# Value products of local and compressed keys on both column halves, their probabilities scaled by DVE

## The chip, the cores and the metric

The kernel runs on one core of one Trainium2 chip. The metric is the device time of one execution in microseconds. Before the change it is 1444.11 us, the median of three runs (1442.19 to 1448.04). Everything is float32.

## The reference

One step of a one-layer decoder for a prompt of 1024 tokens and a sample group of 8 times 4 tokens: an input projection, three kinds of heads side by side (forgetting attention or FoX, sparse attention, HGRN2), an output projection, a norm, and a mixture of experts. The change lies in the attention over the prompt. For each of 4 heads and each block of 128 queries the reference computes there:

```python
# forgetting attention: decay added to the scores, softmax, values
s = q @ k.T * scale + qc[:, None] - kc[None, :]      # causal
o_fox = softmax(s) @ v
# sparse attention: three branches with a gate each
o_c = masked_softmax(q @ kcmp.T * scale + bias) @ vcmp       # compressed keys, up to 63
o_s = masked_softmax(q @ ks.T * scale + bias) @ vs           # selected keys: here all blocks
o_w = masked_softmax(q @ kw.T * scale + bias) @ vw           # local keys: 640 columns at most
o_nsa = g_c * o_c + g_s * o_s + g_w * o_w
```

## The kernel before, in words

TensorE transposes, projects and multiplies; DVE adds biases and takes maxima; ScalarE takes exponentials and copies out of PSUM; GpSimd does some elementwise work and stores. The program of each engine is written out by hand, with semaphores between them.

The attention over the prompt is the stage "attn". It goes through a list of 64 pairs (`PAIRS`): for each head h (4) and each query block i (8), first the pair ("fox", "slc"), which has an even number d, then the pair ("win", "cmp"), which has an odd one. A pair goes through these steps:

1. `scores(d)` on TensorE (L853): products of queries and keys into the ring of four PSUM banks `vec`, at most 512 columns each.
2. `scores(d)` on DVE (L1795): bias added, row minimum taken, result into SBUF.
3. Exponentials on ScalarE (L1377), with their sums.
4. `normalise(d)` on DVE (L1805, L1807): sum times gate, reciprocal: two factors. The probabilities are multiplied by them, for even d by DVE (L1813), for odd d by GpSimd (L2204, which waits for the factors).
5. `transposes(d)` on TensorE (L865) into the three banks `turned`, in blocks of 128 keys.
6. Copies of the transposed probabilities to SBUF on ScalarE (L1370).
7. `values(d)` on TensorE: for even d FoX's products go to partitions 0 to 63 of the one bank `summed` (L877) and those of the selected keys to partitions 64 to 127 (L878), one after the other block by block. For odd d the blocks of local keys (L884, up to 5) and one of compressed keys (L886) are added to partitions 64 to 127 of the same bank.
8. After an odd d ScalarE copies the bank, both halves at once, into `QT` (L1357), and the bank is free.

The steps are staggered. TensorE issues in round d: scores(d), transposes(d-2), values(d-3). ScalarE issues in round d: for odd d-4 the copy out of `summed`, the copies of transposes(d-2), the exponentials of d. DVE issues scores(d), then normalise(d-1). In the round of block 4 of the first three heads TensorE (L841) and DVE (L1771) also make the next head's decay sums, from which GpSimd makes a tile with a mask (L2199) for the next head. The single bank `summed` holds the values of one query block: FoX's values of the next block wait until it has been emptied.

Below, "round E of i" is the even round of query block i, "round O of i" the odd one.

## Time and profile before

| | |
|---|---|
| median of 3 runs | 1444.11 us |
| the profiled execution's own time | 1449.1 us |
| its span, first to last instruction | 1447.0 us |
| TensorE busy in the span | 1304.1 us, 90% |
| the attention stage | about 626 to 891.4 us |
| TensorE, DVE, ScalarE, GpSimd busy in the stage | 240.5, 149.2, 150.8, 68.0 us |
| mean granted TensorE clock, span and stage | 0.94, 0.92 of full speed |

A matrix product of float32 shows as two records of TensorE, each with a weight load of its own. Records overlap at their ends, so the distance between starts says more of their price than their durations.

### The profile page before, as it was taken

To read this page: it belongs to the slowest core of one execution; us is meant where nothing else is said; L and a number is where in the kernel's file an instruction comes from. 1 tells how busy PE (TensorE), PEld (TensorE's weight loads), DVE (VectorE), ACT (ScalarE), POOL (GpSimd) and SP (SyncE) were. 2 spreads that over 40 slices of the span, in tenths; PEclk is the share of its full clock that TensorE was granted. 3 is DMA by queue.
4 is the path that set the end of the run, shared out by engine and by line. 5 is a ranking of instruction groups with operands and counts; after the bars stand their busy time and mean duration, and the time that the engine had idled before them with its cause. 6 is when DMAs were issued, how large, how long until landed. Compare 5 with 4: busy or idle time off the path is not lost.

```text
span 1447.0 us, 19519 instructions
## 1 busy us (share of the span) xinstructions
PE 1304.1 (90%) x6942; PEld 782.1 (54%) x6942; DVE 693.3 (48%) x1565; ACT 405.0 (28%) x858; POOL 237.3 (16%) x273
## 2 busy tenths in 40 slices
PE   3699999999999999878998999999937999999966
PEld 1468787777877555546666656544422333333322
DVE  5526574675744111256565553344762344433329
ACT  2232231422322010135655664222200111111016
POOL 0003021031211000212222222000001222211132
PEclk9799999999999999969999999999957999999988
DMA  9802020130201204306000002520057987595856
GB/s 305 247 26 59 17 73 1 31 59 17 72 2 46 95 9 79 99 12 167 25 21 5 1 1 84 161 80 30 29 199 248 316 287 258 177 319 158 291 177 225
DMA packets 123237, 163.18 MB, mean 113 GB/s; under 512 B 29763, under 2 KB 98547, under 8 KB 123160
## 3 DMA queue, kind: packets, MB, share of 16 engines
q1 hardware_dynamic: 108840, 112.75, 25.5%
q0 software_dynamic: 14320, 49.41, 9.8%
q8 instruction: 48, 0.79, 0.2%
q14 instruction: 29, 0.24, 0.1%
HBM read 225.01 MB, written 36.45 MB: 181 GB/s over the span
## 4 chain that ended last, share of the span: by engine, by line
PE 74%; DVE 16%; POOL 4%; DMA 2%; issue 2%; ACT 2%; SPq 0%; DVEq 0%; POOLq 0%; ACTq 0%
PE act L652 15%; PE vec L1159 11%; PE vec L919 9%; PE vec L681 7%; PE vec L702 4%; POOL arena L2204 3%; DVE arena L1795 3%; PE act L877 3%; PE vec L853 3%; PE act L865 3%; PE act L1172 2%; PE vec L1172 2%; PE vec L817 1%; DMA arena<-x_rows,arena 1%; PE vec L662 1%
## 5 line engine op out<-in xcount | busy, mean ns | idle before, releaser
L652 PE MATMUL act<-arena 128*128 128x352 f32 x768 | 239.1, 467 | 0.4 <-issue 0.4
L652 PEld LDWEIGHTS act<-arena 128*128 128x128 f32 x768 | 145.5, 193 | 77.0 <-issue 3.6
L1159 PE MATMUL vec<-arena 128*64 128x512 f32 x768 | 174.0, 605 | 2.6 <-issue 2.6
L1795 DVE CUSTOM_DVE_ANT_0 arena<-vec,arena 128x128 f32<-128x128 f32 (+9 forms) x200 | 86.8, 459 | 102.7 <-PE vec L853 92.8
L919 PE MATMUL vec<-arena 128*128 128x512 f32 (+1 forms) x288 | 127.8, 599 | 0.4 <-ACT arena L1357 0.4
L1159 PEld LDWEIGHTS vec<-arena 128*64 128x64 f32 x768 | 54.6, 138 | 105.2 <-issue 104.9
L681 PE MATMUL vec<-arena 128*128 128x512 f32 (+1 forms) x256 | 99.9, 546 | 0.0
L1370 ACT COPY arena<-act 128x512 f32<-128x512 f32 (+11 forms) x176 | 63.7, 431 | 105.1 <-PE act L865 105.1
L2204 POOL TENSOR_SCALAR arena<-arena 128x640 f32<-128x640 f32 (+4 forms) x64 | 59.2, 937 | 189.8 <-DVE arena L1807 189.8
L2089 DVE TENSOR_SCALAR arena<-arena 128x256 f32<-128x256 f32 x24 | 7.1, 296 | 172.4 <-ACT arena L1468 172.4
L853 PE MATMUL vec<-arena 64*128 64x512 f32 (+11 forms) x352 | 86.0, 486 | 3.2 <-DVE arena L1795 2.0
L919 PEld LDWEIGHTS vec<-arena 128*128 128x128 f32 (+1 forms) x288 | 51.4, 182 | 68.5 <-issue 66.9
L1377 ACT ACTIVATE arena<-arena 128x640 f32<-128x640 f32 (+15 forms) x128 | 81.5, 643 | 16.2 <-DVE arena L1795 16.1
L865 PE MATMUL act<-arena 128*128 128x128 f32 (+4 forms) x440 | 68.4, 294 | 19.3 <-POOL arena L2204 18.3
L681 PEld LDWEIGHTS vec<-arena 128*128 128x128 f32 x256 | 47.8, 190 | 44.9 <-issue 27.7
L865 PEld LDWEIGHTS act<-arena 128*128 128x128 f32 (+4 forms) x440 | 48.4, 145 | 41.7 <-POOL arena L2204 22.2
L1621 DVE COPY_PREDICATED arena<-arena,vec 128x512 f32<-128x512 int32 x64 | 44.5, 729 | 48.3 <-PE vec L702 46.5
L702 PEld LDWEIGHTS vec<-arena 128*128 128x128 f32 x512 | 61.9, 192 | 9.3 <-DVE arena L1604 3.2
L662 PE MATMUL vec<-arena 128*128 128x128 f32 (+1 forms) x576 | 65.3, 275 | 0.0
L662 PEld LDWEIGHTS vec<-arena 128*128 128x128 f32 (+1 forms) x576 | 64.5, 183 | 1.3
L702 PE MATMUL vec<-arena 128*128 128x128 f32 x512 | 62.7, 276 | 2.4 <-DVE arena L1604 2.4
L2227 POOL DMA_DIRECT2D y_rows<-arena x48 | 25.7, 539 | 229.1 <-DVE arena L2103 228.6
(379 smaller groups left out, 1902.3 us busy)
## 6 DMA issues: line engine op xcount, KB each, us to landing
arena<-in_exp_w SPq DMA_DIRECT2D x144, 1024.0 KB
y_rows<-arena POOLq DMA_DIRECT2D x48, 256.0 KB, 4.9
arena<-in_w_in SPq DMA_DIRECT2D x16, 512.0 KB, 7.1
arena<-in_x_prompt SPq DMA_DIRECT2D x8, 512.0 KB, 10.3
x_spill<-arena POOLq DMA_DIRECT2D x8, 512.0 KB, 6.0
arena<-x_spill SPq DMA_DIRECT2D x8, 512.0 KB, 5.5
arena<-in_cache_fox_kv SPq DMA_DIRECT2D x16, 256.0 KB, 3.5
x_rows<-arena POOLq DMA_DIRECT2D x8, 512.0 KB, 2.9
```

The source lines that it names most:

```text
L652: last = mm(bk[:, 0:n], W[k % 2][:, c, m * P:(m + 1) * P], xT[:, c, a:a + n], start=c == 0, stop=c == NC - 1)
L662: last = mm(bk[:r, o:o + P], xT[:, c, t * P:t * P + r], W[h % 2][:, c, 3 * P:4 * P], start=c == 0, stop=c == NC - 1)
L681: last = mm(bk[:r, 0:width], xT[:, c, t * P:t * P + r], w[:, c, 0:width], start=c == 0, stop=c == NC - 1)
L702: last = mm(bk[:, c * P:(c + 1) * P], a[:, ch], b[:, ch], start=True, stop=True)
L853: mm(bk[:, 0:n], QT[s, h, i * P:(i + 1) * P], k[:, first + a:first + a + n], start=True, stop=True).then_inc(*E.filled("vec"))
L865: last = e.transpose(bk[:n, c * P:(c + 1) * P], score_tiles(d)[j][:, (a + c) * P:(a + c) * P + n], ident)
L919: last = mm(bk[:r], src, Wo[:, c, half * 512:(half + 1) * 512], start=c == 0, stop=c == NC - 1)
L1159: last = mm(gu_bank[p][o], xgT[p][:, c, o], Wgu[:, slot, c, :], start=c == 0, stop=c == NC - 1)
L1370: e.copy(turned_tiles(d)[j][:w, a:a + k, :], bk[:w, 0:k * P].rearrange("p (c n) -> p c n", c=k)).then_inc(*E.drained("turned", ("pt", d, j)))
L1377: act(s, s, ACT.Exp, scale=-1.0, bias=sm_[:, least(i, kind, j):least(i, kind, j) + 1], accum_out=sm_[:, j:j + 1]).then_inc(*E.done(("exps" ...
L1795: ins = e.tensor_tensor_reduce(out=s[:, a + o:a + o + w], in0=bk[:, o:o + w], in1=bias, scale=1.0, scalar=prior, op0=ALU.add, op1=ALU.min, ...
L2204: e.tensor_scalar(s, s, small[:, d % 4, 2 + j:3 + j], None, ALU.mult).then_inc(*E.done(("probs", d)))
```

## The change

The value products of the local keys of an odd pair are parted. About half of them (`own`) stay on partitions 64 to 127 of columns 0 to 127; the rest and the product of the compressed keys go to partitions 0 to 63, columns 128 to 255, of the same bank, and the two kinds are issued in turns. ScalarE copies FoX's part into `QT` and the other half into a new SBUF tile on partitions 64 to 127, with two copies of 64 partitions. DVE then adds that tile to the bank's upper half into `QT` (`add_halves`), which empties the bank. DVE issues the addition at the start of each odd round, ahead of its scores. The scaling of the odd pairs' probabilities moves from GpSimd to the end of `normalise` on DVE.

```diff
--- before.py
+++ after.py
@@ -312,6 +312,7 @@
     PT = [z.take(1024, 8) for _ in range(2)]
     Sw = [[zc.take(640), zc.take(64)] for _ in range(2)]
     PTw = [zp.take(640, 5), zp.take(P, 1)]
+    other_half = zp.take(P)
     assert zc.at <= kept and zp.at <= shared
     assert z.at <= top, (z.at, top)
     attention_end = z.at
@@ -880,10 +881,16 @@
             else:
                 bk = E.banks["summed"][0]
                 first, L, nb = unit_keys("win", i)
-                for c in range(nb):
-                    mm(bk[64:128, 0:P], nkvg[:, first // P + c, 320:384], pt[0][:, c, :], start=False, stop=False)
                 n = unit_keys("cmp", i)[1]
-                mm(bk[64:128, 0:P], VC[:n], pt[1][:n, 0, :], start=False, stop=True).then_inc(*E.filled("summed", ("values", d)))
+                own = nb // 2 + nb % 2
+                upper = [(nkvg[:, first // P + c, 320:384], pt[0][:, c, :]) for c in range(own)]
+                lower = [(VC[:n], pt[1][:n, 0, :])] + [(nkvg[:, first // P + c, 320:384], pt[0][:, c, :]) for c in range(own, nb)]
+                for c in range(max(len(upper), len(lower))):
+                    if c < len(upper):
+                        last = mm(bk[64:128, 0:P], *upper[c], start=False, stop=c == len(upper) - 1)
+                    if c < len(lower):
+                        last = mm(bk[0:64, P:2 * P], *lower[c], start=c == 0, stop=c == len(lower) - 1)
+                last.then_inc(*E.filled("summed", ("values", d)))
 
         E.stage("attn")
         e.wait_ge(*E.at("KC ready"))
@@ -1354,7 +1361,8 @@
                 h, i, _ = PAIRS[d]
                 e.wait_ge(*E.full("summed"))
                 bk = E.job("summed")
-                e.copy(QT[:, h, i * P:(i + 1) * P], bk[:, 0:P]).then_inc(*E.drained("summed", "prompt attention done"))
+                e.copy(QT[0:64, h, i * P:(i + 1) * P], bk[0:64, 0:P]).then_inc(*E.done("fox outputs done"))
+                e.copy(other_half[64:128], bk[0:64, P:2 * P]).then_inc(*E.done(("other half", d)))
             d = it - 2
             if 0 <= d < n:
                 h, i, kinds = PAIRS[d]
@@ -1805,21 +1813,29 @@
             stt(sm_[:, 2:4], sm_[:, 0:2], TINY, skew(GI, 16 * i + 4 * h + 2 * (d % 2), [1, 2]), ALU.max, ALU.mult).then_inc(*E.done())
             e.wait_ge(*E.own())
             e.reciprocal(sm_[:, 2:4], sm_[:, 2:4]).then_inc(*E.done(("factors", d)))
-            if d % 2 == 0:
-                e.wait_ge(*E.own())
-                L = (i + 1) * P
-                for j in range(2):
-                    s = score_tiles(d)[j][:, 0:L]
-                    ts(s, s, sm_[:, 2 + j:3 + j], None, ALU.mult).then_inc(*E.done(("probs", d)))
+            e.wait_ge(*E.own())
+            for j, kind in enumerate(kinds):
+                s = score_tiles(d)[j][:, 0:unit_keys(kind, i)[1]]
+                ts(s, s, sm_[:, 2 + j:3 + j], None, ALU.mult).then_inc(*E.done(("probs", d)))
+
+        def add_halves(d):
+
+            h, i, _ = PAIRS[d]
+            e.wait_ge(*E.full("summed"))
+            bk = E.job("summed")
+            e.wait_ge(*E.at(("other half", d)))
+            tt(QT[64:128, h, i * P:(i + 1) * P], bk[64:128, 0:P], other_half[64:128], ALU.add).then_inc(*E.drained("summed", ("halves added", d), "prompt attention done"))
 
         n = len(PAIRS)
         decay_rows(0)
-        for it in range(n + 1):
+        for it in range(n + 4):
+            if it >= 4 and it % 2:
+                add_halves(it - 4)
             if it < n:
                 scores(it)
                 if it % 16 == 8 and it + 16 < n:
                     decay_rows(it // 16 + 1)
-            if it >= 1:
+            if 1 <= it <= n:
                 normalise(it - 1)
 
 
@@ -2197,11 +2213,6 @@
             if d % 16 == 9 and h + 1 < H:
                 e.wait_ge(*E.at(("cumf", h + 1)))
                 tt(foxdiag[(h + 1) % 2], cumf[(h + 1) % 2].rearrange("p (t k) -> p t k", t=8), C["diagmask"].unsqueeze(1).to_broadcast([P, 8, P]), ALU.add).then_inc(*E.done(("foxdiag", h + 1)))
-            if d % 2:
-                e.wait_ge(*E.at(("factors", d)))
-                for j, kind in enumerate(kinds):
-                    s = score_tiles(d)[j][:, 0:unit_keys(kind, i)[1]]
-                    e.tensor_scalar(s, s, small[:, d % 4, 2 + j:3 + j], None, ALU.mult).then_inc(*E.done(("probs", d)))
         E.stage("p5")
         e.wait_ge(*E.at("prompt attention done"))
         e.wait_ge(*E.at("kv_out"))
```

Two places in the order of the instructions. On TensorE, the end of round E and the start of round O of block 6 of head 2. Before: L853 are scores, L865 transposes, L884 and L886 the values of the local and compressed keys of block 4.

```order
L853 MATMUL vec<-arena 128x512 x2
L853 MATMUL vec<-arena 128x384 x2
L865 MATMUL act<-arena 128x128 x12
L884 MATMUL act<-arena 64x128 x5
L886 MATMUL act<-arena 64x128
```

Now, with L854, L866 for scores and transposes, L890 for the products on the upper half and L892 for those on the lower:

```order
L854 MATMUL vec<-arena 128x512 x2
L854 MATMUL vec<-arena 128x384 x2
L866 MATMUL act<-arena 128x128 x12
L890 MATMUL act<-arena 64x128
L892 MATMUL act<-arena 64x128
L890 MATMUL act<-arena 64x128
L892 MATMUL act<-arena 64x128
L890 MATMUL act<-arena 64x128
L892 MATMUL act<-arena 64x128
```

There are six products as before, now three for each half in turns.

On DVE at the same place, before: L1795 is scores(d) (its rows of 128x1 read out the row minimum), L1805 and L1807 make the factors, L1813 scales.

```order
L1795 ISA arena<-vec,arena 128x384
L1795 ISA arena 128x1
L1805 SCALAR_TENSOR_TENSOR arena<-arena 128x2
L1807 RECIPROCAL arena<-arena 128x2
L1795 ISA arena<-vec,arena 128x512
L1795 ISA arena 128x1
L1795 ISA arena<-vec,arena 128x55
```

Now, with L1803, L1813, L1815 and L1819 for the same four, and L1827 for the addition:

```order
L1803 ISA arena<-vec,arena 128x384
L1803 ISA arena 128x1
L1813 SCALAR_TENSOR_TENSOR arena<-arena 128x2
L1815 RECIPROCAL arena<-arena 128x2
L1819 TENSOR_SCALAR arena<-arena 128x640
L1819 TENSOR_SCALAR arena<-arena 128x47
L1827 TENSOR_TENSOR arena<-act,arena 64x128
L1803 ISA arena<-vec,arena 128x512
L1803 ISA arena 128x1
L1803 ISA arena<-vec,arena 128x55
```

Two scalings and the addition now stand in DVE's queue ahead of the scores of round O.

## Rows read from the trace of the kernel before

**Rows 1.** The page: span, then busy time, share and instructions of TensorE.

```profile
span 1447.0 us, 19519 instructions
...
PE 1304.1 (90%) x6942; PEld 782.1 (54%) x6942; DVE 693.3 (48%) x1565; ACT 405.0 (28%) x858; POOL 237.3 (16%) x273
```

**Rows 2.** Stretches: us, busy per engine, granted clock, DMA share, GB/s.

```profile
626.00:891.40 265.40, 240.45 (x1726) 165.88 (x1725) 149.24 (x623) 150.76 (x465) 68.03 (x69) 0.92 0.12 32
```

**Rows 3.** Waits of the stage: engine and line, releaser, us in total, times, longest.

```profile
DVE arena L1795 <- PE vec L853: 92.8, 61, 3.2
...
PE act L865 <- POOL arena L2204: 18.3, 24, 1.6
```

**Rows 4.** Timeline of TensorE: start, us, line, what.

```profile
769.41 0.92 PE L853 MATMUL vec<-arena 64*128 64x384 f32 x4
...
774.53 0.70 PE L853 MATMUL vec<-arena 64*128 64x512 f32 x2
...
803.82 1.78 PE L853 MATMUL vec<-arena 64*128 64x512 f32 x8
...
813.21 1.13 PE L853 MATMUL vec<-arena 64*128 64x512 f32 x4
...
816.95 1.32 PE L884 MATMUL act<-arena 128*64 128x128 f32 x10
...
818.55 1.57 PE L853 MATMUL vec<-arena 64*128 64x512 f32 x6
...
823.11 0.49 PE L853 MATMUL vec<-arena 64*128 64x128 f32 x4
```

**Rows 5.** Timeline of TensorE: three neighbouring value products, FoX and selected keys.

```profile
792.46 0.27 PE L877 MATMUL act<-arena 128*64 128x128 f32 x1
792.47 0.27 PE L878 MATMUL act<-arena 128*64 128x128 f32 x1
792.57 0.27 PE L877 MATMUL act<-arena 128*64 128x128 f32 x1
```

**Rows 6.** DVE's instructions of the stage by shape: busy us and mean ns.

```profile
L1813 DVE TENSOR_SCALAR arena<-arena 128x768 f32<-128x768 f32 x8 | 4.6, 619 | 0.1
L1813 DVE TENSOR_SCALAR arena<-arena 128x512 f32<-128x512 f32 x8 | 3.5, 485 | 0.1
...
L1813 DVE TENSOR_SCALAR arena<-arena 128x128 f32<-128x128 f32 x8 | 1.9, 286 | 0.1
```

**Rows 7.** GpSimd's instructions of the stage by shape.

```profile
L2204 POOL TENSOR_SCALAR arena<-arena 128x640 f32<-128x640 f32 x16 | 30.1, 1884 | 98.9 <-DVE arena L1807 98.9
...
L2204 POOL TENSOR_SCALAR arena<-arena 128x63 f32<-128x63 f32 x4 | 1.8, 460 | 0.0
```

**Rows 8.** By shape (DVE over the span): the nearest rows for a copy and an addition.

```profile
L1636 DVE SCALAR_TENSOR_TENSOR arena<-arena,vec 128x128 f32<-128x128 f32 x32 | 11.1, 348 | 11.3 <-PE vec L728 10.0
...
L1370 ACT COPY arena<-act 63x128 f32<-63x128 f32 x4 | 1.1, 267 | 0.0
```

**Rows 9.** Timeline of ScalarE: the copy out of the value bank, three times.

```profile
772.56 0.24 ACT L1357 COPY arena<-act 128x128 f32<-128x128 f32 x1
...
809.76 0.28 ACT L1357 COPY arena<-act 128x128 f32<-128x128 f32 x1
...
819.80 0.28 ACT L1357 COPY arena<-act 128x128 f32<-128x128 f32 x1
```

**Rows 10.** Timeline of DVE and GpSimd: two pairs of 640-column scalings.

```profile
791.36 2.76 DVE L1813 TENSOR_SCALAR arena<-arena 128x640 f32<-128x640 f32 x2
...
791.51 2.27 POOL L2199 TENSOR_TENSOR arena<-arena 128x1024 f32<-128x1024 f32 x1
...
853.76 1.02 DVE L1813 TENSOR_SCALAR arena<-arena 128x640 f32<-128x640 f32 x2
```

**Rows 11.** Stretches of 4 us around one fall of the clock.

```profile
776.00:780.00 4.00, 3.20 (x19) 1.87 (x17) 2.93 (x15) 2.44 (x8) 1.58 (x2) 0.99 0.00 0
780.00:784.00 4.00, 3.73 (x21) 2.19 (x20) 0.94 (x3) 1.63 (x6) 0.00 (x0) 0.59 0.00 0
```

## The prediction

> **What bounds the kernel now.** I read the page first. TensorE is busy for 1304.1 of 1447.0 us [rows 1], so a change pays where it takes work or waits off TensorE. Then I cut out the stage that is changed: in 265.4 us TensorE is busy 240.45, DVE 149.24, ScalarE 150.76 and GpSimd 68.03 us [rows 2]. TensorE is the bound there too, with 25 us in which it stands. The waits say for whom: 18.3 us in 24 waits of the transposes (L865) for GpSimd's scaling (L2204), 0.76 us each [rows 3]. In the same rows DVE waits 92.8 us for scores: it has spare time, and so has ScalarE [rows 2]. But both are links of a chain, so their durations count all the same. The last view is TensorE's timeline: it gives the length of a query block from round E to round E, 9.39 us for block 6 (803.82 to 813.21) and 9.90 for block 7 (813.21 to 823.11) [rows 4].
>
> **The value products.** With five blocks of local keys, L884 and L886 take TensorE from 816.95 to 818.55, 1.60 us for six products or twelve records [rows 4]. Where two column halves take turns, one record of each half starts every 0.11 us: L877 at 792.46 and again at 792.57, L878 at 792.47 [rows 5]. The new order is of that form. Six products make three turns of two records, 6 x 0.107 = 0.64 us. The product of the compressed keys uses fewer rows of the array than its neighbours. The twelve records at 0.107 would take 1.28 of the 1.60 us, and I give the other 0.32 to the two changes of form around it and keep it whole: 0.96 us. The gain is 0.64 us for a block, call it 0.62. Sixteen query blocks (i of 4 and more) have this form: 9.9 us. The smaller ones turn 5, 4, 3 and 2 products into 3, 2, 2 and 1 turns, some 0.4, 0.4, 0.2 and 0.2 us by the same working: 1.2 us a head, 4.8 in all. Together 14.7 us off TensorE. Bounds: 0 if the halves don't overlap, and 32 x 0.32 = 10 us more if the changes of form vanished too.
>
> The Trainium skill (TensorE: Matmul & The Clock Gate, Part 3) says that a weight load overlaps running products only where its row group differs. Here both halves use the same rows, so by that rule the turns would save nothing and the sum would lack its 14.7 us. The trace does not agree for this form: two loads and two products fit in 0.11 us.
>
> **The scaling.** GpSimd takes 1884 ns for 640 columns and 460 for 63, together 2.3 us [rows 7]. DVE takes 485 ns for 512 columns and 619 for 768 [rows 6]; for 640 I take the middle, 0.55 us, and for the compressed keys 0.24 (the 128-column row's 286 ns less some columns). The step on the chain shrinks from 2.3 to 0.8 us, 1.5 us less, and the wait is 0.76: it goes, 18.3 us. On DVE the 32 odd pairs cost 4 x (0.29 + 0.35 + 0.42 + 0.49 + 4 x 0.55 + 8 x 0.24) = 22.7 us, in an engine that idles 92.8 for scores. Its cover is thus there, except where something waits behind it in the queue, which comes next. So the most that the change can give is 14.7 + 18.3 = 33 us.
>
> **What is given back: the bank's way out.** The bank `summed` was emptied by one copy of ScalarE, which stands in its queue behind the exponentials of round E. Now two copies stand there and an addition on DVE. A copy with 63 partitions takes 267 ns [rows 8], so the two take 0.52 us. The addition (64x128, one operand in PSUM) isn't in the trace. It can't be less than nothing, since nothing leaves DVE for it, and the nearest row is an operation of two inputs, one in PSUM, on 128x128, 348 ns [rows 8]. I take 0.35 and 0.05 for the handover, as if half the partitions saved nothing. Then FoX's values of round O may begin, and behind them round E of the next block. That makes a loop: E starts, its scores, bias and exponentials pass, the copy begins, and E of the next block starts when copies, addition and values are through.
> - Block 7: the copy began at 819.80, 6.59 us after E [rows 4, 9]. Then 0.92 for copies and addition, 14 x 0.107 + 0.2 = 1.7 for FoX's values of block 6: 9.2 us, against 9.90 now and 9.90 - 0.62 - 0.76 = 8.5 if TensorE alone decided. Gain 0.7.
> - Block 6: 809.76 is 5.94 after E; + 0.92 + 1.5 = 8.35 against 9.39: gain 1.05.
> - Block 2: 772.56 is 3.15 after 769.41; + 0.92 + 0.6 = 4.7 against 5.12 (to 774.53): gain 0.4.
> - Blocks 0, 1, 3 and 5 I estimate from these: 1.1 for block 5, as in block 6; 1.0 for block 3, between its neighbours; 0.5 and 0.3 for blocks 0 and 1, which had no wait for GpSimd or next to none and in which only value products are saved.
>
> Without block 4 that is 5.05 us a head, 20.2 in all, where TensorE alone would allow 29 of the 33. DVE's own queue makes nearly the same loop (the scores of O now stand behind the addition, hence behind ScalarE's exponentials of E), so the two don't add.
>
> **Block 4.** In the first three heads GpSimd makes the next head's tile there (L2199). DVE's scalings of 640 columns began at 791.36, GpSimd's operation at 791.51 for 2.27 us, and the two scalings took 2.76 us; in the last head, without it, two took 1.02 [rows 10]. DVE stood still until GpSimd was through. Before, GpSimd's own scaling came first. Now its queue is empty, it starts as soon as the sums are there, and DVE's scaling of block 3's odd pair, 0.2 us later, waits for its end. The transposes of that pair come 0.5 us later than now instead of earlier, and the addition and the scores of O stand behind it. I take a loss of 0.5 us for each of three heads and a gain of 1.2 for the last: -0.3 in all.
>
> The Trainium skill (SBUF — State Buffer, Who interferes with whom) has the rule for it: a scaling on DVE in a two-port mode and a GpSimd operation lock each other out for a whole instruction. By that rule block 4 costs what I give it above, where an unhindered DVE would gain 1.2 us in each of three more heads, 5 us of the sum; rows 10 agree. The rule also says that an operation with at most one SBUF input is free of it, so the addition would not wait; no row here shows that.
>
> **The sum.** 20.2 - 0.3 - 0.6 (at the end of the stage the output projection waits for the second copy and the addition) = 19.3, say 19. What follows the stage starts from it and shifts whole. The profiled execution took 1449.1 us: 1430.1. The median of the runs was 5.0 us lower: 1425.
>
> **Rivals.**
> - *TensorE decides everywhere.* If the copies and the addition hide, 33 us come: 1411. For it: ScalarE and DVE are busy little more than half of the stage. Against: the loop's lengths above.
> - *The new loop is longer than I have it.* The exponentials of E start later because DVE is late from the round before; 0.4 us more in each of 32 blocks takes 13 us: gain 6, 1438. For it: DVE gets 22.7 us of scaling and 32 x 0.35 = 11 us of additions.
> - *The halves do not overlap*, since the compressed keys' product uses other rows. 18.3 us of waits go, less what the loop takes, and 8 us are left: 1436. Against: rows 5.
> - *Slower: the clock.* The granted clock was 0.59 from 780 to 784, after 3.20 us of 4 busy from 776 to 780 [rows 11], which is the lower level (1.2 GHz) for most of 4 us and costs 1.7 us of work at full speed. The packed products leave TensorE with fewer of them and more of it as transposes. Were there one more in each of 28 blocks, 48 us would be lost against 33 won: 1459. It decides from 11 more on. Against: the long gaps in front of it go.
>
> **How the numbers follow.** Forecast 0.60, TensorE alone 0.10, longer loop 0.13, no overlap 0.11, clock 0.06. A measurement here tells some 0.5% (7.2 us, so 1436.9) from no change. Faster: 0.60 + 0.10 + a third of the longer loop's 0.13 + half of the 0.11 = 0.80. Slower: 0.06. The rest, 0.14, is the same. The range reaches from TensorE alone (1411) to the longer loop (1438): 1412 to 1438, with the clock's case and the ends of the others outside.
>
> **What would show it.** In the profile after: no scaling on GpSimd in the stage and no wait of the transposes for it; the records of the two halves starting in couples 0.11 us apart; DVE busy 178 us there or a little less; a wait of FoX's values or of DVE's addition for ScalarE's copies; block 6 at 8.3 us; a long scaling on DVE beside GpSimd's tile in three heads; a stage of some 246 us instead of 265. I am wrong if the records of the halves start one by one, if the stage keeps its length, or if the mean clock in it falls under 0.90.

## The result

| | before | after |
|---|---|---|
| median, us | 1443.69 (4 runs, 1442.19 to 1448.04) | 1430.45 (4 runs, 1422.10 to 1431.61) |
| ratio, 95% interval | | 0.9891 (0.9848 to 0.9934) |
| profiled execution, us | 1449.1 | 1430.46 |

The changed kernel is faster by 1.1%. Timed again beside the last experiments, on one chip with them, the ratio was 0.9897 (0.9880 to 0.9914). The forecast was 1425 us, in a range of 1412 to 1438. The range held the time, and the ratio stands for 16 us where 19 were forecast.

The page of the kernel after: span and TensorE's line, as [rows 1] of before.

```profile
span 1428.5 us, 19615 instructions
...
PE 1289.3 (90%) x6942; PEld 765.9 (54%) x6942; DVE 721.5 (51%) x1661; ACT 414.8 (29%) x890; POOL 177.7 (12%) x209
```

The span is 18.5 us shorter. The stage now goes from 626 to 873 us (TensorE's first product of the output projection starts at 872.96, before at 891.37). This row of the stretches answers to [rows 2]: length, busy time of TensorE, weight loads, DVE, ScalarE and GpSimd, granted clock, DMA share, GB/s.

```profile
626.00:873.00 247.00, 226.75 (x1724) 150.65 (x1722) 176.95 (x717) 160.79 (x497) 8.04 (x5) 0.95 0.13 34
```

18.4 of the 18.5 us are in this stage. DVE is busy 177 us where 178 were forecast. The clock is 0.95 where it was 0.92. Next the waits of the same stretch, as [rows 3]: total us, times, longest.

```profile
PEld act L866 <- DVE arena L1819: 23.3, 25, 2.0
DVE arena L1827 <- ACT arena L1365: 22.4, 15, 4.0
...
DVE arena L1803 <- PE vec L854: 13.7, 16, 2.5
...
PE act L866 <- DVE arena L1819: 9.9, 8, 1.8
```

GpSimd's scaling is gone from the list; one wait of DVE for GpSimd, 2.1 us, is there before and after. DVE waits 13.7 us for scores instead of 92.8, and has a new wait: 22.4 us of its addition for ScalarE's second copy. TensorE's transposes wait 9.9 us, for DVE, where they waited 18.3 for GpSimd. Their weight loads (PEld) are idle as long as before, 23.3 against 22.2 us, yet only 8 of these 25 times do the products stand too (24 of 24 before). Of the 9.9 us, 5.5 lie in block 4 of the first three heads and 2.8 in block 0 of the last three.

The length of a block is the distance between the scores of two even rounds. These rows are TensorE's timeline of head 2 (the heads count from 0), as [rows 4]: the even rounds of blocks 6 and 7, the first of FoX's value products in block 7, then the even round of the next head's block 0 and its transposes.

```profile
789.77 1.78 PE L854 MATMUL vec<-arena 64*128 64x512 f32 x8
...
798.28 1.99 PE L854 MATMUL vec<-arena 64*128 64x512 f32 x8
...
805.95 0.29 PE L878 MATMUL act<-arena 128*64 128x128 f32 x1 [0.25 <-DVE arena L1827]
...
807.64 0.49 PE L854 MATMUL vec<-arena 64*128 64x128 f32 x4
809.00 1.20 PE L866 MATMUL act<-arena 128*128 128x128 f32 x9 [0.86 <-DVE arena L1819]
```

Block 6 takes 8.51 us (789.77 to 798.28), forecast 8.35; block 7 takes 9.36, forecast 9.2. In block 7 the value products stand 0.25 us for the addition; in block 6 TensorE stands for nothing. And in the last row TensorE stands 0.86 us for the scaling of block 7, which no rival of mine had in this place. The way out of the bank in the same blocks, first ScalarE's copies (as [rows 9]), then DVE's additions with what they waited for:

```profile
795.72 0.26 ACT L1364 COPY arena<-act 64x128 f32<-64x128 f32 x1
796.00 0.26 ACT L1365 COPY arena<-act 64x128 f32<-64x128 f32 x1
...
804.87 0.26 ACT L1364 COPY arena<-act 64x128 f32<-64x128 f32 x1
805.15 0.26 ACT L1365 COPY arena<-act 64x128 f32<-64x128 f32 x1
```

```profile
796.36 0.29 DVE L1827 TENSOR_TENSOR arena<-act,arena 64x128 f32<-64x128 f32 x1 [1.16 <-ACT arena L1365]
...
805.51 0.29 DVE L1827 TENSOR_TENSOR arena<-act,arena 64x128 f32<-64x128 f32 x1 [1.53 <-PE act L866]
```

The copies begin 5.95 and 6.59 us after the even round, as before (5.94 and 6.59). The addition ends 6.88 us after the round in block 6, forecast 5.94 + 0.92 = 6.86. In block 7 it ends at 805.80 and the first value product starts at 805.95: this second handover of 0.15 us has no term in the forecast, and it is nearly all that the two blocks are longer than forecast (0.16). The engine named last in such a row is not always the one that released: at 805.51 it is the copy that ended at 805.41.

The value products of five blocks of local keys and the compressed ones, in the last block of the last head:

```profile
866.25 0.43 PE L890 MATMUL act<-arena 128*64 128x128 f32 x2
866.61 0.43 PE L892 MATMUL act<-arena 55*64 55x128 f32 x2
866.97 0.32 PE L890 MATMUL act<-arena 128*64 128x128 f32 x1
866.97 0.32 PE L892 MATMUL act<-arena 128*64 128x128 f32 x1
867.13 0.27 PE L890 MATMUL act<-arena 128*64 128x128 f32 x1
...
867.56 0.33 PE L866 MATMUL act<-arena 128*128 128x128 f32 x1
```

The first couple does not overlap: two records of L890, then from 0.36 us later two of L892 with 55 rows, again 0.36 us, and only then couples, 0.16 and then 0.11 us apart, as [rows 5]. Six products take 1.31 us (866.25 to 867.56), before 1.60, forecast 0.96 to 0.98.

DVE's new operations (shape, count, busy us and mean ns, as [rows 6, 8]) and one of three meetings with GpSimd, as [rows 10]:

```profile
L1819 DVE TENSOR_SCALAR arena<-arena 128x640 f32<-128x640 f32 x24 | 12.9, 553 | 0.7
...
L1819 DVE TENSOR_SCALAR arena<-arena 128x512 f32<-128x512 f32 x12 | 10.2, 880 | 0.3
...
L1827 DVE TENSOR_TENSOR arena<-act,arena 64x128 f32<-64x128 f32 x32 | 9.5, 296 | 38.0 <-ACT arena L1365 22.4 <-PE act L866 11.2 <-PE vec L854 4.3
```

```profile
716.77 2.21 DVE L1819 TENSOR_SCALAR arena<-arena 128x512 f32<-128x512 f32 x2
...
716.55 2.00 POOL L2215 TENSOR_TENSOR arena<-arena 128x1024 f32<-128x1024 f32 x1 [60.45 <-DVE arena L1813]
```

640 columns take 553 ns (forecast 0.55), the addition 296 (taken as 350), but two scalings that should take 0.64 us take 2.21 beside GpSimd's tile, until it ends.

**All blocks.** I took the block lengths of every head from TensorE's scores, as above. Where the clock doesn't fall inside them they repeat to 0.02 us from head to head, with two exceptions after: block 0 takes 8.02 in head 1 and 7.85 in the next two, block 5 7.95 in head 1 and 8.04 in the last. In this table are those undisturbed lengths of heads 1 to 3 in us; block 4 is that of the last head, which has no tile and no sums. A star marks a length with a stretch at the lower clock in it, for want of another.

| kernel | 0 | 1 | 2 | 3 | 4, last head | 5 | 6 | 7 | 4, other heads |
|---|---|---|---|---|---|---|---|---|---|
| before | 7.21 | 4.10 | 5.12 | 6.27 | 8.41* | 8.88 | 9.39 | 9.90 | 11.83* and more |
| after | 7.85 | 4.05 | 4.91 | 5.71 | 6.89 | 8.0 | 8.51 | 9.37 | 11.13 |
| scaling by DVE alone | 7.22 | 4.10 | 4.32 | 5.40 | 6.69 | 8.03 | 8.79 | 9.33 | 11.12 |
| value part alone | 7.31 | 4.04 | 5.13 | 6.27 | 8.46* | none | 9.39 | 9.90 | 10.89 |
| after, addition behind the scores | 7.06 | 4.53 | 4.94 | 6.33 | 7.51 | 8.74 | 9.31 | 9.87 | 12.96* |
| after, early copies | 7.05 | 3.89 | 4.37 | 5.54 | 6.62 | 7.96 | 8.50 | 9.04 | 12.30* and more |
| after, late tile | 7.85 | 4.03 | 4.91 | 5.72 | 6.89 | 7.95 | 8.51 | 9.37 | 9.55 |
| scaling by DVE, late tile | 7.22 | 4.10 | 4.32 | 5.40 | 6.69 | 8.03 | 8.79 | 9.33 | 9.55 |
| after, all three edits | 7.03 | 3.73 | 4.37 | 5.20 | 6.47 | 7.60 | 8.35 | 8.89 | 9.55 |

From before to after, blocks 0 to 3 and 5 to 7 gain 2.5 us a head, 10 us in four. Three things correct this.

- Block 4: the 8.41 us of the last head before have 1.5 us at the lower clock in them. Less half of that they are 7.66, an estimate, and the gain is 0.8. In the other heads the same working gives 10.8 to 10.9 before against 11.13 after, a loss of some 0.3 in each of three.
- The stage's end: from the last even round on it takes 19.36 us where it took 18.03. It loses 1.3 us where block 7's gain of 0.5 stands in the 10. The transposes of the last odd pair wait 1.28 us for DVE's scaling there.
- The first two blocks of head 0 run at the lower clock and gain 0.4 together where the table has a loss of 0.6.

That leaves some 9 of the 18.4 us. The rest is the clock, told below.

### The profile page after: what moved, and what is told of

Read it like the earlier page. It is cut to its first block, busy times and chain, and to the rows that moved or that the text cites. A ratio compares the mean times of both kernels' runs of the same rounds, so it can differ in the third digit from the quotient of the medians.

```text
span 1428.5 us, 19615 instructions
## 1 busy us (share of the span) xinstructions
PE 1289.3 (90%) x6942; PEld 765.9 (54%) x6942; DVE 721.5 (51%) x1661; ACT 414.8 (29%) x890; POOL 177.7 (12%) x209
## 4 chain that ended last, share of the span: by engine, by line
PE 77%; DVE 14%; DMA 3%; ACT 3%; issue 2%; POOL 0%; SPq 0%; DVEq 0%; POOLq 0%; ACTq 0%
PE act L653 15%; PE vec L1166 11%; PE vec L926 9%; PE vec L682 7%; PE vec L854 5%; PE vec L703 4%; PE act L866 4%; PE act L878 2%; PE act L1179 2%; PE vec L1179 2%; DMA arena<-x_rows,arena 2%; PE vec L818 1%; PE act L890 1%; PE vec L663 1%; PE act L1146 1%
## 5 line engine op out<-in xcount | busy, mean ns | idle before, releaser
L1803 DVE CUSTOM_DVE_ANT_0 arena<-vec,arena 128x128 f32<-128x128 f32 (+9 forms) x200 | 86.8, 459 | 25.3 <-PE vec L854 13.7
L854 PE MATMUL vec<-arena 64*128 64x512 f32 (+11 forms) x352 | 84.2, 477 | 2.3 <-DVE arena L1803 1.8
L866 PE MATMUL act<-arena 128*128 128x128 f32 (+4 forms) x440 | 66.3, 288 | 10.9 <-DVE arena L1819 9.9
L866 PEld LDWEIGHTS act<-arena 128*128 128x128 f32 (+4 forms) x440 | 47.2, 142 | 31.9 <-DVE arena L1819 23.3
L854 PEld LDWEIGHTS vec<-arena 64*128 64x128 f32 x352 | 42.5, 197 | 33.4 <-issue 18.3
L1476 ACT ACTIVATE arena<-vec 128x256 f32<-128x256 f32 x24 | 9.3, 386 | 165.9 <-PE vec L1166 165.9
## 6 DMA issues: line engine op xcount, KB each, us to landing
arena<-in_x_prompt SPq DMA_DIRECT2D x8, 512.0 KB, 10.2
```

The lines of the kernel that those rows point to most:

```text
L854: mm(bk[:, 0:n], QT[s, h, i * P:(i + 1) * P], k[:, first + a:first + a + n], start=True, stop=True).then_inc(*E.filled("vec"))
L866: last = e.transpose(bk[:n, c * P:(c + 1) * P], score_tiles(d)[j][:, (a + c) * P:(a + c) * P + n], ident)
L1803: ins = e.tensor_tensor_reduce(out=s[:, a + o:a + o + w], in0=bk[:, o:o + w], in1=bias, scale=1.0, scalar=prior, op0=ALU.add, op1=ALU.min, ...
```

## The experiments

The theories: A, the one on record, that the wait for GpSimd is won and the longer way out of the value bank limits the gain; B, that the packed value products bring it; C, that a large part is the clock. The code below is shortened; what each line does stands in the text around it.

### Each part alone

The first kernel has DVE's scaling only (GpSimd's goes, as in the change; the line that scales stays as it was):

```diff
-            if d % 2 == 0:
-                e.wait_ge(*E.own())
-                L = (i + 1) * P
-                for j in range(2):
-                    s = score_tiles(d)[j][:, 0:L]
+            e.wait_ge(*E.own())
+            for j, kind in enumerate(kinds):
+                s = score_tiles(d)[j][:, 0:unit_keys(kind, i)[1]]
```

> The kernel before with one part of the change: DVE scales the probabilities of the odd pairs; value products, the single copy and GpSimd's empty queue otherwise as before. Theory A (the forecast's: the wait for GpSimd is what the change takes away): the 18.3 us of waits go, block 6 takes 8.9 us instead of 9.39, block 7 9.4 instead of 9.90, time 1430 to 1434. Rival B (the packed value products bring most): 1440 or more. Rival C (most of the gain is the clock, which falls less often when the waits are gone): 1430 too, but blocks without a fall gain under 0.4 us each and the stage shows 3 falls or fewer instead of 7.

It took 1421.51 us, ratio 0.9871 (0.9847 to 0.9895). TensorE's even rounds of blocks 5, 6 and 7 in the last head:

```profile
829.21 1.56 PE L853 MATMUL vec<-arena 64*128 64x512 f32 x8
...
837.24 1.78 PE L853 MATMUL vec<-arena 64*128 64x512 f32 x8
...
846.03 1.99 PE L853 MATMUL vec<-arena 64*128 64x512 f32 x8
```

Block 5 lasts 8.03 us, block 6 8.79 and block 7 9.33 (in the table), the last two 0.1 less than theory A has them. The time is 9 us lower than I expected of A. Some 4 us of that lie ahead of the stage, where the kernels are the same: in this trace its first product starts at 622.2 us, in that of the changed kernel at 626.4. A stage read from a trace is thus a better measure than the time when kernels of different series are compared, and it says more here: 264.7 us before, 246.5 with the whole change, 241.8 with the scaling alone. Of rival C's two conditions one holds and one does not: the stage has a single fall of the clock (counted as told below), but undisturbed blocks 2, 3, 5, 6 and 7 gain 0.6 to 0.9 us each too. Both theories hold a part.

The second kernel has the rest: value products on both halves, two copies, the addition, and GpSimd's scaling.

```diff
+            if d % 2:
+                e.wait_ge(*E.at(("factors", d)))
+                for j, kind in enumerate(kinds):
+                    s = score_tiles(d)[j][:, 0:unit_keys(kind, i)[1]]
+                    e.tensor_scalar(s, s, small[:, d % 4, 2 + j:3 + j], None, ALU.mult).then_inc(*E.done(("probs", d)))
```

> The other part alone: value products on both halves with two copies and DVE's addition, the odd pairs still scaled by GpSimd. Theory A: TensorE comes earlier to transposes that wait for GpSimd anyway, so the waits grow by what the products save and the longer way out of the bank costs a little: 1440 to 1448. Rival B (products bring most): 1434 or less. Rival C (clock): falls as often as before, 7 in the stage, and 1440 to 1446.

1444.55 us, ratio 1.0011 (0.9991 to 1.0030): nothing, as A said, and B falls. C's numbers hold nearly as well as A's (8 falls of the clock where 7 were named). Its transposes still wait for GpSimd (from 640 to 830 us):

```profile
PE act L866 <- POOL arena L2222: 15.1, 17, 1.6
```

So all the gain is in the scaling, and the value part on top of it takes some back. The two ratios with and without it (0.9891 and 0.9871) don't tell this apart, the block lengths do: in the table 1.2 us a head between those rows and 0.2 more in the last head's block 4, 5 us in all (blocks 0, 2 and 3 pay 1.5, block 6 wins 0.28 back). The stages of the two traces differ by 4.8 us. With a later edit in both kernels (the late tile, below) the ratios tell it too: 0.9842 (0.9816 to 0.9868) against 0.9774 (0.9755 to 0.9793).

### The product with fewer rows

```diff
-                lower = [(VC[:n], pt[1][:n, 0, :])] + [(nkvg[...], pt[0][:, c, :]) for c in range(own, nb)]
+                lower = [(nkvg[...], pt[0][:, c, :]) for c in range(own, nb)] + [(VC[:n], pt[1][:n, 0, :])]
```

> The changed kernel with the product of the compressed keys last among those on the lower half instead of first. In the changed kernel this product and its neighbour on the upper half run one after the other. If its odd number of rows costs a change of form on either side, putting it last takes one of them away: L890 and L892 together take 1.1 us for a block instead of 1.3. Theory A (the way out of the bank sets the length of a block): the time doesn't move beyond 1 us, blocks 6 and 7 stay at 8.5 and 9.4. Rival (TensorE's own work sets it): 0.2 us in each of 28 blocks, 5 us.

1423.85 us, ratio 0.9883 (0.9856 to 0.9910), not told apart from the changed kernel's by these intervals. Six products now take 1.16 us (853.01 to 854.17 in its trace) against 1.31, and blocks 6 and 7 stay at 8.50 and 9.36: less work of TensorE does not shorten them. It does shorten blocks 0 and 5, by 0.1 and 0.2 us (7.74, and 7.72 or 7.84).

```diff
-                lower = [(VC[:n], pt[1][:n, 0, :])] + ...
+                lower = [(nkvg[:, 0, 320:384], pt[0][:, 0, :])] + ...
```

> The changed kernel with a block of local keys (128 rows) multiplied a second time in the place of the compressed keys, whose values are left out of the result. If the number of rows keeps the first couple from overlapping, all couples now start 0.11 us apart and six products take 0.64 to 0.8 us instead of 1.3. If the place (first on the half) is to blame, nothing changes. Blocks 6 and 7 keep their 8.5 and 9.4 us in theory A and lose 0.5 us if TensorE's own work sets them.

One execution, 1426.27 us; in it the values of the compressed keys are left out, a sixth local product stands for them. In its trace the six products of the last head's block with five blocks of keys, and the scores behind them:

```profile
855.06 0.32 PE L890 MATMUL act<-arena 128*64 128x128 f32 x1
855.06 0.32 PE L892 MATMUL act<-arena 128*64 128x128 f32 x1
855.22 0.27 PE L890 MATMUL act<-arena 128*64 128x128 f32 x1
...
855.87 0.69 PE L854 MATMUL vec<-arena 64*128 64x512 f32 x1
```

They start as couples from the first on and take 0.81 us (855.06 to 855.87), 0.16 of it at the start of the form and 0.22 at its end. So it is the number of rows, not the place on the half, that keeps the first couple apart. And with 0.5 us less work in TensorE blocks 6 and 7 still take 8.51 and 9.37. What was saved comes back as a wait of FoX's values for DVE's addition, 0.44 us in block 6 and 0.76 in block 7 of head 2:

```profile
803.97 0.29 PE L878 MATMUL act<-arena 128*64 128x128 f32 x1 [0.76 <-DVE arena L1827]
```

That settles it: the bank's way out lets these blocks become no shorter.

### The way out of the bank

```diff
-            if it >= 4 and it % 2:
-                add_halves(it - 4)
             if it < n:
                 scores(it)
+            if it >= 4 and it % 2:
+                add_halves(it - 4)
```

> The changed kernel with DVE's addition of an odd round behind the scores of that round instead of ahead of them. Block lengths of the changed kernel are 7.85, 4.05, 4.91, 5.71, 6.89 (last head), 8.0, 8.5, 9.37 us in all heads. If DVE's queue sets them (the scores stand behind an addition that waits for ScalarE's copies, which stand behind the exponentials), the scores run as soon as TensorE has them and blocks 2, 3, 6 and 7 come down to about 4.4, 5.4, 8.2 and 8.9 us: 1423 or less. If the bank's way out sets them (theory A as forecast), the addition comes no earlier than now and all stay: 1428 to 1431.

1442.76 us, ratio 1.0005 (0.9987 to 1.0023). The one line's place is worth all that the change brings. I had "DVE's queue" and "the bank" as rivals, and expected at worst no change. The trace shows why there is one; first ScalarE's second copy, then DVE's scores of the odd round and the addition:

```profile
856.38 0.26 ACT L1365 COPY arena<-act 64x128 f32<-64x128 f32 x1
```

```profile
856.38 0.69 DVE L1803 CUSTOM_DVE_ANT_0 arena<-vec,arena 128x512 f32<-128x512 f32 x1 [0.51 <-PE vec L854]
...
857.38 0.35 DVE L1803 CUSTOM_DVE_ANT_0 arena<-vec,arena 128x128 f32<-128x128 f32 x1
...
857.77 0.30 DVE L1827 TENSOR_TENSOR arena<-act,arena 64x128 f32<-64x128 f32 x1
```

The copy is done at 856.64. The addition could start there but stands behind the odd round's scores until 857.77, 1.1 us later, so the bank is empty 1.1 us later; the addition ends at 858.07, and FoX's values begin at 858.21. DVE then waits 57.2 us for scores in the stage (13.7 in the changed kernel). Blocks 6 and 7 take 9.31 and 9.87, nearly what they took in the kernel before (9.39 and 9.90). The bank's way out is the loop that decides, and the addition's place ahead of the scores is right.

```diff
                 for j, kind in enumerate(kinds):
+                    if j == 1:
+                        copy_out(it - 3)
```

`copy_out` holds the two copies, which before stood at the start of ScalarE's round it + 1.

> The changed kernel with ScalarE's two copies between the two exponentials of the even round instead of behind both: they are done 0.5 to 1 us earlier, and the second exponential 0.5 us later. Both theories of the loop (bank, DVE's queue) expect shorter blocks: 8.3 and 9.0 us for blocks 6 and 7, 1423 to 1427. If the blocks are set by TensorE's work or by the exponentials' end, nothing or a loss of 0.5 us a block.

1422.42 us, ratio 0.9873 (0.9852 to 0.9894). That is 2.6 to 3.5 us better than the changed kernel by the ratios (0.9891 and 0.9897), with intervals that overlap; the blocks add up to 2.05 us a head and 0.27 in the last head's block 4, 8.5 us in all. The stages differ by 2.7 us only (246.5 and 243.8), in part since this one spent 8 us more at the lower clock. ScalarE's timeline in block 6 of the last head (exponentials L1391, copies L1364 and L1365):

```profile
846.42 1.08 ACT L1391 ACTIVATE arena<-arena 128x896 f32<-128x896 f32 x1
...
847.45 0.26 ACT L1364 COPY arena<-act 64x128 f32<-64x128 f32 x1
847.73 0.26 ACT L1365 COPY arena<-act 64x128 f32<-64x128 f32 x1
848.02 1.04 ACT L1391 ACTIVATE arena<-arena 128x896 f32<-128x896 f32 x1
```

The copies now begin 4.9 us after the even round (842.53) instead of 5.95. Block 0 gives back the 0.8 us that it had lost, blocks 2, 3, 4 and 7 give 0.54, 0.17, 0.27 and 0.33. Block 6 stays at 8.50, against my expectation of 8.3: TensorE's own work is 9.39 less its old wait of about 0.53 and the 0.29 of the packed products, 8.57, and in this trace it stands for nothing in blocks 5 to 7. In block 6 of the changed kernel the two limits lie on one another: neither less work of TensorE nor an earlier bank shortens it, and both together do (8.35 in the fastest kernel below).

> Both: copies between the exponentials, addition behind the scores. If DVE's queue alone decides, no better than the kernel with the later addition alone; if both links do, blocks 6 and 7 at 8.1 and 8.7 us and 1418 to 1422. As fast as DVE's scaling alone (1421.5) or faster only if the packed products' 0.3 us a block come through.

This kernel has both edits, the late addition and the early copies. 1442.38 us, ratio 1.0007 (0.9991 to 1.0024), with the block lengths of the late addition to 0.01 us. My expectation missed: once the addition stands behind the scores, it is they that hold the bank, and the copies may come when they like.

### The tile of the next head

```diff
                 e.wait_ge(*E.at(("cumf", h + 1)))
+                e.wait_ge(*E.at(("probs", d)))
```

> The changed kernel, but GpSimd makes the next head's tile after DVE has scaled the odd pair of block 4 instead of as soon as the sums are there. If the two engines lock each other out, the three scalings of 512 columns that took near 2 us take 0.49 and block 4 of the first three heads (11.1 us without a fall of the clock) becomes 1.3 us shorter, 4 us in all, provided that the operation doesn't hit another scaling. If block 4 is set by the sums and not by the scaling, nothing.

1419.04 us, ratio 0.9842 (0.9816 to 0.9868), the changed kernel and one line. DVE's scalings of block 3 (512 columns) and of the odd pair of block 4, and GpSimd's tile:

```profile
714.62 0.64 DVE L1819 TENSOR_SCALAR arena<-arena 128x512 f32<-128x512 f32 x2
...
721.50 0.71 DVE L1819 TENSOR_SCALAR arena<-arena 128x640 f32<-128x640 f32 x2
...
722.35 2.00 POOL L2216 TENSOR_TENSOR arena<-arena 128x1024 f32<-128x1024 f32 x1 [56.07 <-DVE arena L1819]
```

Two scalings take 0.64 us where they took 2.21, and the tile, which starts when the last one is done, meets none. Block 4 of the first three heads goes from 11.13 to 9.55, 1.58 us each where 1.3 were expected. 4.7 us follow from that. The ratio stands for 7 to 8 us, and its four executions spread from 1415.03 to 1426.15, the profiled one being the slowest, so the rest is not settled; the stage of that one is 5.8 us shorter than the changed kernel's. From 632 us on it had no fall of the clock.

### The clock

The granted clock of 190 us in the middle of the stage (columns as above), in this order: before, the changed kernel, the scaling alone, the value part alone, the scaling with the late tile (the next experiment), and the early copies:

```profile
640.00:830.00 190.00, 173.67 (x1260) 121.41 (x1261) 109.55 (x444) 108.47 (x331) 50.00 (x49) 0.93 0.16 44
```

```profile
640.00:830.00 190.00, 175.68 (x1352) 117.13 (x1350) 140.09 (x565) 124.96 (x391) 6.01 (x3) 0.97 0.16 44
```

```profile
640.00:830.00 190.00, 182.05 (x1393) 126.63 (x1391) 137.53 (x556) 121.90 (x374) 6.00 (x3) 0.98 0.16 44
```

```profile
640.00:830.00 190.00, 170.68 (x1279) 114.53 (x1277) 116.85 (x479) 115.95 (x365) 49.98 (x51) 0.95 0.16 43
```

```profile
640.00:830.00 190.00, 186.61 (x1454) 130.42 (x1453) 139.10 (x579) 126.74 (x388) 6.00 (x3) 1.00 0.16 43
```

```profile
640.00:830.00 190.00, 181.19 (x1367) 120.53 (x1366) 142.16 (x570) 127.27 (x395) 5.99 (x3) 0.95 0.16 44
```

0.93, 0.97, 0.98, 0.95, 1.00 and 0.95. Each fall to the lower level (1.2 GHz) is a clock record of its own in the trace; from 632 to 880 us there are 7 in the kernel before, 2 after, 1 with the scaling alone, 8 with the value part alone and none with the late tile. One of the usual length costs a block 1.6 to 1.8 us: block 5 of the kernel before took 8.88 us without, 10.49 to 10.67 with one.

But the records differ in length, and each stage begins at the lower level. So the time at that level, added up from the records of each trace, says more than their number:

| kernel | stage, us | at the lower level, us | of it after the stage's first 40 us |
|---|---|---|---|
| before | 264.7 | 41.0 | 20.5 |
| after | 246.5 | 22.6 | 3.4 |
| scaling by DVE alone | 241.8 | 20.5 | 0 |
| value part alone | 264.9 | 41.0 | 23.9 |
| after, addition behind the scores | 262.3 | 32.1 | 13.7 |
| after, late addition and early copies | 263.9 | 37.5 | 14.1 |
| after, early copies | 243.8 | 30.7 | 10.2 |
| after, late tile | 240.8 | 17.1 | 0 |
| scaling by DVE, late tile | 231.6 | 11.7 | 0 |
| after, all three edits | 224.7 | 12.5 | 0 |

From before to after it is 18.4 us less. At half the speed that is 9 us of the 18.4, where TensorE is what the stage waits for; this is an estimate, not a measurement by itself, and it fits what the blocks leave over. Kernels in which TensorE's waits shrank spent 8 to 31 us of the stage at the lower level (the traces not in the table counted too), those in which they stayed 32 to 41. The early copies are the case against a simple rule: TensorE's waits of over 0.15 us add up to 24.0 us of the stage before, 18.9 after and 12.2 with the early copies, but the time at the lower level went 41.0, 22.6, 30.7. Why a fall comes the traces do not show.

### What is fastest

The first of these has the edit of the scaling alone and that of the late tile:

```diff
                 e.wait_ge(*E.at(("cumf", h + 1)))
+                e.wait_ge(*E.at(("probs", d)))
```

> DVE's scaling alone (value products and single copy as in the kernel before) and GpSimd's tile after the scaling of block 4. In the trace of DVE's scaling alone TensorE doesn't stand at all in blocks 5 to 7 (8.03, 8.79, 9.33 us). Expected: these unchanged, block 4 of the first three heads 9.6 instead of 11.1 us: 4.6 us less than the 1421.5, 1417.

It took 1411.21 us, ratio 0.9774 (0.9755 to 0.9793). The blocks are as expected and block 4 takes 9.55 us; the time is 6 us lower than expected. Against the scaling alone, from which I had reckoned, the trace has 8.8 us less at the lower level, worth some 4, and a start of the stage 1.2 us earlier.

In the second the single copy out of the bank stands between the exponentials, as above.

> The one above with the single copy out of the value bank between the two exponentials. Since TensorE doesn't stand for the bank in blocks 5 to 7, nothing there; if the bank still holds back the small blocks 2 to 4, some 0.2 us each, under 3 us in all: 1415 to 1418. If an earlier copy helps whatever bounds the block, 0.5 us a block, 1405.

1411.49 us, ratio 0.9778 (0.9762 to 0.9794), no block changed by more than 0.02 us. With the single copy the bank holds nobody back.

The third is the changed kernel with three edits shown above: the compressed keys' product last, the early copies and the late tile.

> The changed kernel with the copies between the exponentials, the compressed keys' product last and GpSimd's tile after the scaling of block 4; the addition stays ahead of the scores. From the block lengths of the three single edits (7.05, 3.9, 4.37, 5.54, 6.6 or 9.3, 7.8, 8.5, 9.04 us): 9 us less from the copies and 4.7 from the tile than the changed kernel: 1415. If the packed products are worth something once the way out is short, it beats DVE's scaling with the late tile by 3 us; if not, the two are equal.

1404.96 us, ratio 0.9726 (0.9708 to 0.9744), the fastest of all, and 10 us lower than expected. Some 4 of them lie ahead of the stage, which starts at 622.3 us here and at 626.4 in the trace that I had reckoned from; 10 us less at the lower level are worth some 5.

```profile
span 1400.9 us, 19618 instructions
...
PE 1275.3 (91%) x6942; PEld 759.4 (54%) x6942; DVE 718.2 (51%) x1661; ACT 415.3 (30%) x890; POOL 177.3 (13%) x209
```

Once the way out is short, the packed products are worth something: blocks 5, 6 and 7 take 7.60, 8.35 and 8.89 us against 8.03, 8.79 and 9.33 without them, 1.3 us a head, the stages of the two traces are 224.7 and 231.6 us long, and the two intervals of the ratio are apart (0.9708 to 0.9744, 0.9755 to 0.9793). Last, the changed kernel once more.

> The changed kernel itself on the chip of the three above, for comparison. Both theories: 1428 to 1431, with block lengths as in its first trace to 0.1 us and only the number of falls of the clock different; if that number varies by two or three between runs, single runs vary by some 4 us.

1429.58 us, ratio 0.9897 (0.9880 to 0.9914), block lengths as in its first trace to 0.03 us, but for disturbed ones, and again 2 falls. In both traces the falls lie at the same places of the stage. The single runs lay within 1.6 us here; in the first series one of 1422.10 us had a mean clock of 0.956 where the three others had 0.947 to 0.949.

## Why the prediction was right, and where it was not

- *The wait for GpSimd goes.* Right; the scaling alone brings 1.3% (1.1 to 1.5), all that the whole change brings. But of the 18.3 us of waits 9.9 came back as waits of the transposes for DVE's scaling, of which the forecast had only those in block 4.
- *DVE's scalings: 22.7 us, 0.55 for 640 columns; the addition 0.35.* Right: 0.553, and 0.296 for the addition, a little less than taken.
- *The way out of the bank sets the length of blocks 6 and 7: 8.35 and 9.2.* Right for block 7 (9.37), and shown by taking away TensorE's work (the block kept its length and TensorE waited for the addition instead) and by delaying the addition (the blocks grew by 0.8 and 0.5). In block 6 (8.51) it is half of the truth: TensorE's own work is as long, 8.50, where the forecast's terms give 9.39 - 0.62 - 0.76 = 8.0. The method, old distance of the copy from the round plus the new steps, held because the steps up to the copy did not move; a second handover of 0.15 us was missing.
- *The value products: 0.62 us a block, 14.7 in all.* Mis-sized. They save 0.29 us a block of five, since the product with fewer than 128 rows doesn't overlap with its neighbour and costs a change of form on both sides. I had counted two such changes and the couple as overlapped. The rival "the halves do not overlap" had this reason right, for one couple in three. With 128 rows the term is 0.8 (1.60 to 0.81). In the sum it did little harm, since the loop allowed no more in blocks 6 and 7.
- *Blocks 0 and 1: gains of 0.5 and 0.3.* Wrong for block 0, which loses 0.64 and has a long wait that is new, 0.86 to 1.03 us of the transposes for DVE's scaling. The same wait, 1.28 us, stands in the stage's end, which takes 1.3 us longer than before. I followed only the bank into this block. DVE arrives late from block 7, where the addition had waited for ScalarE, and has scores, two factors and 1.4 us of scaling still in front of the transposes. With the early copies at most 0.29 us of the wait are left and the block takes 7.05, which bears this out. Block 1 gained 0.05. Blocks 2, 3 and 5 gained 0.2, 0.55 and 0.9, forecast 0.4, 1.0 and 1.1. Together the seven blocks gained 2.5 us a head, forecast 5.05.
- *Block 4: a loss of 0.5 in three heads.* The mechanism is right and shown (2.21 us against 0.64 beside the tile). The loss itself can't be read off, since the kernel before has a fall of the clock in each of these blocks; the estimate above puts it at some 0.3 each, and the last head's gain at 0.8, forecast 1.2. With the value part alone, where GpSimd still scales first, the block took 10.89, against 11.13 after.
- *The clock.* I had it as a rival that would slow the kernel down. It did the opposite: some 9 us of 18.4 go with 18.4 us less at the lower level. The sum of 19 was met by luck: two errors offset each other, 10 us too much for the blocks and 9 too little for the clock. The direction was argued rightly (the gaps go), but given no term.

## What to carry to other kernels

Before timing a change of two parts, time each part: here one gave all the gain, and the other cost 1.2 us a head until its way out was shortened, and only then paid. A step that frees a single buffer belongs as early as it can be issued on every engine that it passes, and its place in the queue can be worth more than its work. Where TensorE stands for a microsecond here and there, look at the granted clock of that stretch: in these traces the stages with shorter waits mostly spent less time at the lower level, and that was worth about as much as the waits. Compare the stages of two traces, not only the times: here up to 5 us of a difference lay ahead of the changed stage.

## What the runs showed of the hardware

- A product with fewer rows than its neighbour on the other column half (55 or 63 against 128) did not overlap with it; with 128 rows on both it did, 1.31 against 0.81 us for six.
- DVE's scaling of 512 columns stood still while GpSimd's operation on 1024 columns ran: two scalings took 2.21 us against 0.64. GpSimd's own operation took 2.00 us beside it, as it did without a scaling beside it; in the kernel before, where DVE's scalings had begun first, it took 2.27 [rows 10].
- One fall of the clock cost 1.6 to 1.8 us of a block that is bound by TensorE. With shorter waits of TensorE the time at the lower level went from 41.0 to 22.6 us of the stage, and to 12.5 in the fastest kernel; with the early copies it was 30.7, though the waits were shorter still. What exactly sets a fall off stays open here.
- From the end of DVE's addition to the first product of TensorE that waited for it 0.15 us passed (805.80 to 805.95).
